# A hybrid decoder layer on one core: five of eight projected chunks go into a stage of their own beside expert rows, and keys and values go through memory

## What is computed

```
proj = rms_norm(x, norm_mix) @ w_in                 # 1024 x 2208: c_q 384, c_kv 256, k_rope 32, dq, dk, dv 512 each
q  = rms_norm(c_q) @ w_uq ; kv = rms_norm(c_kv) @ w_ukv ; rope on q and k_rope
h  = x + [gnorm(mla_attention) ; gnorm(dilated_attention)] @ w_out        # causal, 8 + 8 heads
h  = h + memory_attention(rms_norm(h), rms_norm(mem))                     # 4 heads, 256 memory tokens
xn = rms_norm(h)
s  = (xn @ w_q) . sub_keys                            # 8 heads x 2 x 128 scores
best 16 of 128 twice, best 16 of the 256 sums -> 16 experts per head, 128 per token
h  = h + sum over the 128 picks of softmax(best) * gelu(xn . peer_u[expert]) * peer_v[expert]
out = rms_norm(h, norm_final)
```

## Time and profile before

| | us |
|---|---|
| median of 3 runs | 4009.39 (3992.87 to 4014.03) |
| the profiled execution | 3997.09 |
| its span, first to last instruction | 3995.3 |
| fold_weights | 0 to 192.6 |
| project_tokens, chunks 0 to 7 | 192.6 to 585.6 |
| attend, chunks 0 to 2 | 585.6 to 749.6 |
| pick_chunks 0 to 2 | 749.6 to 1316 (first gather 847.5) |
| attend, chunks 3 to 7 | 1316 to 2071.9 |
| pick_chunks 3 to 7 | 2071.9 to 3995.3 |

### The profile page before, as it was taken

The page is one execution under the profiler, slowest core; times in us unless marked ns, Lnnn a source line. Parts: engine busy times, 40 slices in busy tenths (PEclk is TensorE's granted clock), DMA queues, the critical chain, the costliest instruction groups (busy, mean ns, idle before and its releaser), DMA issues. The chain is left out here.

```text
span 3995.3 us, 35611 instructions
## 1 busy us (share of the span) xinstructions
PE 3069.8 (77%) x9134; PEld 1570.6 (39%) x9134; DVE 2429.8 (61%) x5667; ACT 1320.0 (33%) x3405; POOL 1373.9 (34%) x1367
## 2 busy tenths in 40 slices
PE   8799988758686778887868878778777787866665
PEld 6644445323232335444434433333333333322222
DVE  0311112166837667766743787887887788788765
ACT  1211113211111234334323453543444444344333
POOL 0000000023544566666642333333333333333332
PEclk9899997778888798899989989999999999998999
DMA  7710012489987889999988999999999999999998
GB/s 290 264 39 24 24 69 89 147 299 341 349 320 265 320 317 357 377 328 339 354 342 331 378 399 417 403 415 420 411 407 404 412 412 415 421 416 401 421 419 349
DMA packets 283759, 1288.88 MB, mean 323 GB/s; under 512 B 27440, under 2 KB 52144, under 8 KB 193072
## 3 DMA queue, kind: packets, MB, share of 16 engines
q0 software_dynamic: 195120, 1073.83, 68.1%
q1 hardware_dynamic: 83696, 195.62, 13.6%
q10 hardware_dynamic: 4752, 17.30, 1.2%
HBM read 1243.65 MB, written 42.99 MB: 322 GB/s over the span
## 5 line engine op out<-in xcount | busy, mean ns | idle before, releaser
L495 PE MATMUL e_acc<-s_ring,s_diagonal 128*128 128x512 f32 x2296 | 976.0, 555 | 451.3 <-ACT s_diagonal L323 389.2
L393 DVE CUSTOM_DVE_ANT_0 s_ring<-s_ring,e_x_copy 128x1024 f32<-128x1024 f32 x581 | 706.9, 1217 | 283.0 <-DMA s_ring<-peer_uv,s_expert 215.4
L495 PEld LDWEIGHTS e_acc<-s_ring,s_diagonal 128*128 128x128 f32 x2296 | 426.1, 201 | 1057.7 <-ACT s_diagonal L323 626.1
L277 POOL DMA_INDIRECT s_ring<-peer_uv,s_expert x462 | 437.0, 946 | 792.2 <-DVE e_part L426 586.6
L277 POOL DMA_INDIRECT s_ring<-peer_u,s_expert x331 | 361.2, 1091 | 428.5 <-DVE s_expert L1706 238.5
L495 PE MATMUL e_acc<-e_more_slots,s_diagonal 128*128 128x512 f32 (+1 forms) x948 | 383.2, 531 | 149.9 <-ACT s_diagonal L323 140.9
L323 ACT ACTIVATE s_diagonal<-s_ident,s_gate 128x128 f32<-128x128 f32 x1024 | 396.4, 398 | 264.2 <-PE e_acc L495 138.8
L340 ACT ACTIVATE s_dots<-s_dots 128x1 f32<-128x1 f32 x704 | 142.2, 202 | 979.4 <-DVE s_dots L393 976.1
L277 POOL DMA_INDIRECT s_ring<-peer_v,s_expert x325 | 343.1, 1056 | 355.1 <-PE e_acc L495 128.8
L277 POOL DMA_INDIRECT e_more_slots<-peer_uv,s_expert x231 | 218.0, 944 | 403.1 <-DVE e_part L426 282.8
L393 DVE CUSTOM_DVE_ANT_0 e_more_slots<-e_more_slots,e_x_copy 128x1024 f32<-128x1024 f32 x231 | 281.6, 1219 | 110.8 <-DMA e_more_slots<-peer_uv,s_expert 107.6
(11 more groups left out here) (204 smaller groups left out, 3719.0 us busy)
## 6 DMA issues: line engine op xcount, KB each, us to landing
e_halves<-peer_scores SPq DMA_DIRECT2D x12, 2048.0 KB
e_halves<-mem_scores SPq DMA_DIRECT2D x6, 2048.0 KB
e_halves<-mem_values SPq DMA_DIRECT2D x6, 2048.0 KB
...
peer_scores<-f_stage_s SPq DMA_DIRECT2D x16, 512.0 KB, 4.7
...
```

The lines of the kernel that those rows point to most:

```text
L277: pool.indirect_dma_start(out=to, out_offset=None, in_=table, in_offset=bass.IndirectOffsetOnAxis(ap=self.expert[c % PICK_BUFFERS][:, k:k ...
L393: dve.tensor_tensor_reduce(row, row, x[:, :], 1.0, 0.0, ALU.mult, ALU.add, self.dots[:, k:k + 1]).then_inc(self.u_used, 1)
L495: last = pe.matmul(self.acc[:, at:to], self.diagonal[:, made % DIAGONALS, :], row[:, at:to], start=(n == group[0]), stop=(n == group[-1]))
```

## The change

- `project_tokens` takes a range of chunks. It runs for 0 to 2 alone, at the old place, and again for 3 to 7 as a stage of its own ("woven") between the picks of 0 to 2 and the attention of 3 to 7, beside rows 150 to 300. `ROWS_BESIDE` puts 30 rows a chunk at eight places of the engines' programs: 8 before c is normed, 10 after it, 2, 4, 1, 2, 1 and 2 behind the later steps.
- In that stage a v row has 0 columns on TensorE: VectorE adds all 1024 columns into `s_h`, and ScalarE makes no diagonals. The accumulators of the projection take the whole PSUM.
- Keys and values no longer stay on chip over the stages: each chunk's are stored (kept_mla_k, kept_dil_k, kept_values), and the attention of 3 to 7 loads all of them at its start, behind eight rows (`HEAD_ROWS`).
- w_in, w_uq and w_ukv, multiplied with their gains, are stored in the first projection and loaded again in the second.
- With `keep` gone from the chip, the picks of 0 to 2 hold the tables whole, loaded once; the half slots are gone.
- The picks of 0 to 2 now lie beside rows 0 to 150 (chunk 0's and 1's to row 45 and 90), the attention of 3 to 7 beside rows 300 to 640. Rows 640 to 2048 are as before.
- The hardware loops over chunks are written out.

The diff, cut to its core:

```diff
-            pe += kind == "v"
+            pe += kind == "v" and self.columns[s] > 0
...
-                    pool.wait_ge(self.v_pe, self.pe_through[m])
+                    if self.pe_columns(m) > 0:
+                        pool.wait_ge(self.v_pe, self.pe_through[m])
...
+        if self.pe_columns(last) == 0:
+            dve.wait_ge(self.v_dve, self.dve_through[last])
+            dve.sem_inc(self.h3_ready, 1)
+            return
...
-def project_tokens(nc, io, keep, ahead):
+def project_tokens(nc, io, first, end, ahead=None, keep=None, stream=None, until=0):
...
+            ROWS_BESIDE = (8, 10, 2, 4, 1, 2, 1, 2)
+            start = stream.at["vector"]
+            shares = np.cumsum(np.tile(ROWS_BESIDE, COUNT))
+            rows_until = [start + int(c) for c in np.floor((until - start) * shares / shares[-1])]
...
+        def kept(t):
+            at = slice(0, P) if woven else slice(P * t, P * (t + 1))
+            to = slice(P * (first + t), P * (first + t + 1))
+            i = 0 if woven else t
+            return ((keep["mla_k_t"][0:QK, :, at], io["kept_mla_k"][0:QK, :, to]),
+                    (keep["dil_k_t"][:, :, at], io["kept_dil_k"][:, :, to]),
+                    (keep["values"][:, i, :], io["kept_values"][:, first + t, :]))
...
+            if woven:
+                load_x(0)
+                for t in range(DT):
+                    sp.dma_start(w_in[:, t, :], io["w_in_gained"][:, t, :]).then_inc(w_in_loaded[t], 16)
...
+            for t in range(COUNT):
+                if t + 1 < COUNT:
+                    sp.wait_ge(x_normed, t + 1)
+                    load_x(t + 1)
+                if not woven:
+                    store_weights(range(t * (DT + 2) // COUNT, (t + 1) * (DT + 2) // COUNT))
                 sp.wait_ge(dq_t_ready, t + 1)
+                sp.dma_start(io["dil_q_t"][first + t], dq_out[:, :, :]).then_inc(dq_stored, 16)
+                mla, dil, values = kept(t)
+                sp.wait_ge(dk_t_ready, t + 1)
+                sp.dma_start(dil[1], dil[0]).then_inc(kv_stored, 16)
+                sp.wait_ge(dv_ready, t + 1)
+                sp.wait_ge(v_ready, t + 1)
+                sp.dma_start(values[1], values[0]).then_inc(kv_stored, 16)
                 sp.wait_ge(q_t_ready, t + 1)
-            with sp.Fori(0, CHUNKS - 1) as t:
-                sp.wait_ge(x_normed, t + 1)
-                sp.dma_start(x_rows, io["x"][bass.ds((t + 1) * P, P), :]).then_inc(x_loaded, 16)
-                store_queries(t)
-            store_queries(CHUNKS - 1)
-            sp.wait_ge(dq_stored, 16 * CHUNKS)
-            sp.wait_ge(q_stored, 16 * CHUNKS)
+                sp.dma_start(io["mla_q_t"][first + t], q_out[:, :, :]).then_inc(q_stored, 16)
+                sp.wait_ge(k_t_ready, t + 1)
+                sp.dma_start(mla[1], mla[0]).then_inc(kv_stored, 16)
+            sp.wait_ge(dq_stored, 16 * COUNT)
+            sp.wait_ge(q_stored, 16 * COUNT)
...
+                mla_k, dil_k, values = (on_chip for on_chip, _ in kept(t))
+                values = values.unsqueeze(1)
+                if woven:
+                    beside(stream.vector, t, 0)
...
+                if woven:
+                    beside(stream.vector, t, 1)
                 if more:
                     norm_x(t + 1)
+                if woven:
+                    beside(stream.vector, t, 2)
+                    need(dve, kv_stored, 48 * t)
+                dve.wait_ge(v_projected, t + 1)
+                dve.tensor_copy(values[:, :, WIDTH:2 * WIDTH], pair_d[:, 0:BANK].unsqueeze(1)).then_inc(dv_ready, 1)
+                if woven:
...
+            if woven:
+                dve.wait_ge(small_loaded, 32)
...
+                    if woven:
+                        pe.wait_ge(w_in_loaded[k], 16)
...
-            rows_until = [start + int(c) for c in np.floor((until - TAIL - start) * np.cumsum(weights) / weights.sum())]
+            HEAD_ROWS, TAIL = 8, 8
+            begin = start + HEAD_ROWS
+            rows_until = [begin + int(c) for c in np.floor((until - TAIL - begin) * np.cumsum(weights) / weights.sum())]
...
+            if stream is not None:
+                sp.dma_start(keep["mla_k_t"][0:QK, :, :], io["kept_mla_k"][0:QK, :, :]).then_inc(keep_loaded["mla_k_t"], 16)
             load_table(0)
+            if stream is not None:
+                sp.dma_start(keep["values"][:, :, :], io["kept_values"]).then_inc(keep_loaded["values"], 16)
+                sp.dma_start(keep["dil_k_t"][:, :, :], io["kept_dil_k"]).then_inc(keep_loaded["dil_k_t"], 16)
...
+            if stream is not None:
+                stream.tensor(begin)
+                pe.wait_ge(keep_loaded["mla_k_t"], 16)
             score(0)
             score(1)
+            if stream is not None:
+                pe.wait_ge(keep_loaded["values"], 16)
+                pe.wait_ge(keep_loaded["dil_k_t"], 16)
             for n, (t, u, nb) in enumerate(ALL_UNITS):
...
-        last = resident
-        HALVES = ([("mem_scores", BANK * i) for i in range(2)] + [("mem_values", BANK * i) for i in range(2)] +
-                  [("peer_scores", BANK * i) for i in range(4)])
-        HALF_SLOTS = 3
-        if resident:
+        if last:
             stream.more_slots = sb("e_more_slots", [P, WIDE_RING - RING, D])
-            mem_scores = sb("e_mem_scores", [P, DT, D])
-            mem_values = sb("e_mem_values", [P, DT, D])
-            peer_scores = sb("e_peer_scores", [P, DT, 2 * D])
-            tables_loaded = [sem(f"e_tables_loaded{i}") for i in range(3)]
-        else:
-            halves = sb("e_halves", [P, HALF_SLOTS, DT, BANK])
-            half_loaded = [sem(f"e_half_loaded{i}") for i in range(HALF_SLOTS)]
-        b = pick_buffers(sb, ps, sem, stream, resident)
+        mem_scores = sb("e_mem_scores", [P, DT, D])
+        mem_values = sb("e_mem_values", [P, DT, D])
+        peer_scores = sb("e_peer_scores", [P, DT, 2 * D])
+        tables_loaded = [sem(f"e_tables_loaded{i}") for i in range(3)]
+        b = pick_buffers(sb, ps, sem, stream, last)
         gain_kept = chunks[0] == 0
...
-PICK_02, ATTEND_37 = 215, 640
-STAGES = [(PICK_02, "pe", D), (ATTEND_37, "split", BANK), (len(ROWS), "pe", 3 * D // 4)]
-FRONTS = [(ATTEND_37, 705), (712, 894), (914, 1148), (1170, 1404), (1426, 1660)]
+FIRST = 3
+FIRST_TWO = 90
+PICK_FIRST, PROJECT_REST, ATTEND_REST = 150, 300, 640
+STAGES = [(PICK_FIRST, "pe", D), (PROJECT_REST, "split", 0), (ATTEND_REST, "split", BANK), (len(ROWS), "pe", 3 * D // 4)]
...
+            third = [(at, 2, name) for at, _, name in one_by_one([FIRST_TWO + 1], PICK_FIRST)]
+            pick_chunks(nc, io, stream, [0, 1, 2], first_two(FIRST_TWO) + third, PICK_FIRST, False)
+            project_tokens(nc, io, FIRST, CHUNKS, stream=stream, until=PROJECT_REST)
+            sb, _, _ = allocators(nc, ctx, "_rest", side="right")
+            keep = keys_and_values(sb, SEQ)
+            attend(nc, io, keep, FIRST, CHUNKS, stream.ident, stream, ATTEND_REST)
```

237 lines of the change are left out of this document (138 added, 99 removed).

## The result

The changed kernel takes 3891.7 us (median, 3886.39 to 3898.64); the kernel before, beside it, 4002.14 (3992.87 to 4014.03). The ratio is 0.9732, 95% interval 0.9709 to 0.9756: 110 us or 2.7% faster, where some 50 (1.3%) were forecast. On a second chip the ratio was 0.9741 (0.9718 to 0.9764). The sign was right and the time lies in the range; the size was not. In the spans of the profiled executions the gain is 98.5, where the sum of the prediction had 43.

What follows compares the result with a forecast made beforehand. Taken as bounds: idle DMA before the first row, the picks' own work, near-balanced engines in projection and attention, DMA last. 618 + 400 + 326 + 686 = 2030, plus 1922, 2 and a third of 12: 3958 us, range 3880 to 4040.

Steps and rivals of the forecast that it cites:

- The last stage and the frame: Picks of 3 to 7, rows 640 to 2048, at the DMA limit: 1922 us as before, and 2 around the span.
- The dead time: Before a row's first dot product, DMA mostly idle: five fewer projected chunks, 47.4 us each, bring it from 854.7 to 618.
- the 610 within 10: Announced profile sign: the first gather of an expert's row starts at 610 us, within 10.
- The picks: Picks of 0 to 2 beside 150 rows instead of 215, set by the picks, not the rows: 400 us, bounds 375 and 420.
- the two stalls: VectorE's two 13.7 us waits before x overwrites h2, its store behind table reloads; half of 26.3, 13, taken off the picks.
- the last dot before 990: Announced sign: last dot of the picks at 1018; before 990 would mean VectorE's own work did not bound them.
- The new stage: Projection of 3 to 7 beside 150 rows: start 38, five chunks of 56, chunk 0's end 8, together 326 us.
- Attention: Attention of 3 to 7 beside 340 rows instead of 425: start 50, body 610, tail 26, together 686 us, bounds 640 and 735.
- A: Rival, 0.17: engines have room in the projection beside rows; chunk 50, attention body 565, 8 off the picks: 3875 us.
- B: Rival, 0.15: attention does not shrink with its rows, TensorE's hand-overs set its body at 657: total 3998 to 4005 us.
- C: Rival, 0.10: rows beside the projection do not hide, about 81 us a chunk, 125 more: total 4083 us.
- D: Rival, 0.06: GpSimd's gather issue, at 2.0 + 0.3 each, bounds the projection beside rows, 69 us a chunk: total 4020.

Runs made afterwards that it cites:

- Experiments 3: Kernel before, with the projection's loops over the eight chunks written out on all engines: 3982.53 us, ratio 0.9964 to the kernel before.
- experiment 10: Kernel before with loops written out, next x's norm ahead of the copy of v, h2 store issued from ScalarE: 3956.07 us, ratio 0.9896.
- experiment 2: Changed kernel with tables of the picks of 0 to 2 again reloaded in 2 MB halves, not resident: 3925.57 us, ratio 0.9806 to kernel before.
- experiment 9: Changed kernel, unedited, run again on a second chip: 3894.75 us, ratio 0.9741 to the kernel before.
- experiment 12: Changed kernel with 40 rows moved from attention to picks, first 512 tokens' keys and values loaded first, cosines and sines ahead of w_in: 3920.88 us, ratio 0.9799.
- experiment 6: Changed kernel, loading keys and values of the first 512 tokens first at attention's start, the rest behind the queries: 3886.13 us, ratio 0.9747.
- experiment 4: Changed kernel with each projected chunk's 30 rows in one block at its end instead of eight places: 4062.91 us, ratio 1.0163 to kernel before.
- experiment 7: Changed kernel with dot products in the picks of 0 to 2 reading x from SBUF instead of its PSUM copy: 3885.17 us, one run.

## Why the prediction was right in sign and half the size

**The last stage and the frame** held: no other stage than those named moved.

**The dead time, 618 against 602.** Two causes. I priced a chunk alone at 47.4 from the kernel before and kept that price for the three that stay. The diff writes the loops out and puts the norm of the next x ahead of the copy of v; both stand in it in plain sight and neither had a term. Experiments 3 and 10 give 1.7 and 1.4 for them. The stage is 243 shorter, not 237: the two full periods between the three key copies give 6, the first chunk 2 more, and the stage's end takes 2 back, since its last key store, which the prediction put at 0, is waited for (5.8 from the last key copy's end to SP's next load, 3.6 before). The first attention is 2 shorter. The rest, 8, is the first picks, whose length the prediction kept: the wait of 8.6 ahead of chunk 0's x, outside, was put at 0, and x now starts 5.0 after h2 instead of 13.6. The first dot at 602.1 is the earliest of all runs; in the others with whole tables it came at 605.7 to 609.2, so part of the 8 is luck. The first gather came at 597.5, outside the 610 within 10 that was announced.

**The picks, 400 against 381.** This is the step that failed most. The prediction saw the two stalls, 26.3 in all, behind reloads, and then "the store itself remains, so I take half off". Nothing in the profile said half: the only row on a transfer of this size has 512 KB landing in 4.7, and the store's landing runs beside VectorE's norm. What remained is 1.2, so the half was 12 too little. The other 7 of the 19 were not tracked down: experiment 2 gives 5 more than the waits for the tables in halves, and the picks of the same kernel vary by 11 among the profiles, with 380.8 the longest. One count in the term was off as well: chunk 2's front loses 18 rows (50 to 32), not 16, which is 1 us. The blocks in which experts are chosen, bound by VectorE's own work, were right within 1, and the last dot before 990, which the prediction named as the sign of a wrong limit, came for this reason and not for that one.

**The new stage, 326 against 306.6.** Head 38 against 37.6. A chunk is 54 against 56, by two errors that partly cancel, which is luck: alone it costs 44.2, not 47.4, but sharing costs 10, not 5 plus 3 to 4. Of the 10 the trace of experiment 9 shows 6.2 between the copy of v and the next chunk's first product (20.5 against 14.3 alone), the hand-overs of the tail, and 1.7 in the next chunk's first product, which follows such a wait at a granted clock of 0.84 and takes 11.0 instead of 9.3. In the same way the product of p_c_t with p_w_uq takes 5.8 instead of 4.1 (part of the 6.2), at 0.72. Some 2 of the 10 are not placed. From its first to its last dot the stage is 269.1, where 288 stood. The three middle chunks are 9 less. The first is 8 less, 48 from the first row to its key copy's end, because its products start inside the head, with a piece of w_in at 1005. The last, 64.8 with chunk 0's end in it, is as forecast (56 + 8). Another 3.5 lie behind the last dot, where the forecast counted whole chunks.

**Attention, 686 against 683.9.** The sum was right because two errors cancel. The head to the body was 38 (1289.6 to 1328) instead of 50: mla_k was waited for 12.6, not behind all 14.3 MB. The body was 620 instead of 610. Whether TensorE and DMA weigh the same in it, as the prediction said, is open: DMA is 0.91 busy, experiment 12 is at most a hint that the body follows TensorE's clock, and in experiment 6 a shorter head is given back where DMA is full.

**The rivals.** A (3875) was nearer to 3891.7 than the forecast. Its mechanism, that all three engines have room in the new stage, held, but both of its prices failed (a chunk of 50 against 54, an attention body of 565 against 620), so its nearness is luck. B fell: 101 rows fewer took 97 off the body, 0.96 each. C is not what happened, and experiment 4 shows that its price was real, 172 for its 125. D fell in its size: 1.31 a gather where 2.0 would have been needed, and experiment 7 shows that such contention exists.

**The whole miss.** 55 in the span: 16 in the dead time (6, 2 and 8), 19 in the picks, 19 in the new stage, 2 in attention, less 1 in the last stage. By cause, the h2 stall is some 18 of it (12 in the picks, some 6 net in the first picks). The shorter chunk alone is some 22 (6, and 5 x 3.1 in the new stage), of which the dearer sharing took some 6 back. The first chunk's start inside the head and the way the stage's end is counted are 8 and 3.5. Both large items are side effects of the diff that I read and priced by half or not at all. The 62 of experiment 10 for moving the chunks, with the tables, lie above what the forecast had for the same: of its 51, 13 were the stall, so 38 against some 50 without the stall's rest.
